# Hybrid decoder step with product-key experts, one core: h copied into PSUM in 36 of 64 expert steps, and projection heads, query norms, diagonals and late attention moved

## The reference, cut to what matters

```
q   = h @ w_pq, split in 8 heads x 2 halves x 128; each half normalised
s   = q . sub_keys                      (128 keys per half)
16 best of each half -> 16 x 16 sums -> 16 best: expert e = i1 * 128 + i2
gate = softmax(16 best sums)
act  = gelu(h . expert_u[e])            (16 experts per head and token)
out += gate * act * expert_v[e]         -> second layer norm -> y
```

## Time and profile before

| what | value |
|---|---|
| median of 3 runs | 4193.62 us |
| span of the profiled execution | 4435.8 us |
| POOL busy | 2465.2 us (56%) |
| DVE busy | 2799.8 us (63%) |
| PE busy | 2995.1 us (68%) |
| gathers of expert rows | 2 x 1024, and 16 for the sample |

### The profile page before, as it was taken

One profiled execution on the slowest core, in us unless ns is written; L12 is line 12 of the kernel. 1 busy time (PEld: TensorE's weight loads), 2 busy tenths in 40 slices (PEclk: granted clock), 3 DMA queues, 4 the chain that ended last, 5 costly groups with the idle time before them and its releaser, 6 DMA issues.

```text
span 4435.8 us, 41900 instructions
## 1 busy us (share of the span) xinstructions
PE 2995.1 (68%) x12168; PEld 1491.0 (34%) x12168; DVE 2799.8 (63%) x6694; ACT 917.6 (21%) x2005; POOL 2465.2 (56%) x2288
## 2 busy tenths in 40 slices
PE   5968877976866777866677778885666654444435
PEld 3546545645414433422223334441222221010001
DVE  6576851324665466668766766666776668657662
ACT  1423110233411244421111134331111110000000
POOL 1010110102576565676777777667777767777775
PEclk8988988966687877877888888767878877777777
DMA  6575983336699888899999999889999999999998
GB/s 234 182 310 218 386 328 104 106 126 215 230 360 348 313 312 285 306 345 359 370 378 386 362 358 354 326 309 332 380 376 375 382 357 338 354 362 360 348 342 310
DMA packets 422338, 1388.96 MB, mean 313 GB/s; under 512 B 46374, under 2 KB 124454, under 8 KB 409822
## 3 DMA queue, kind: packets, MB, share of 16 engines
q0 software_dynamic: 306432, 1216.48, 73.2%
q1 hardware_dynamic: 89390, 140.65, 9.4%
q10 hardware_dynamic: 26288, 29.15, 1.9%
HBM read 1333.57 MB, written 56.86 MB: 313 GB/s over the span
## 4 chain that ended last, share of the span: by engine, by line
POOL 35%; PE 15%; issue 15%; DMA 5%; DVE 4%; another core or an unknown queue 4%; DVEq 1%; ACT 0%; ACTq 0%; SPq 0%; PEldq 0%; POOLq 0%; PEld 0%
POOL st_rows L1525 35%; DMA st_rows<-in_peer_v,st_expert_v 4%; PE st_ps_q L1794 3%; PE st_ps_m L1804 3%; PE st_ps_q L1833 2%; PE st_ps_y L1878 2%; PE st_ps_t L1777 2%; DVE st_rows L2113 1%; PE st_ps_m L1810 1%; DMA st_rows<-in_peer_u,st_expert 1%; PE st_ps_m L1746 1%; PE st_ps_q L1797 1%; PE st_ps_s L1862 1%; DMA st_h<-scr_h 0%
## 5 line engine op out<-in xcount | busy, mean ns | idle before, releaser
L1878 PE MATMUL st_ps_y<-st_rows,st_diag 128*32 128x512 f32 x4096 | 1095.6, 658 | 730.7 <-DMA st_rows<-in_peer_v,st_expert_v 633.1
L1525 POOL DMA_INDIRECT st_rows<-in_peer_u,st_expert x1024 | 1191.3, 1163 | 645.4 <-issue 292.3
L2113 DVE CUSTOM_DVE_ANT_0 st_rows<-st_rows,st_h 128x1024 f32<-128x1024 f32 x1024 | 1218.1, 1223 | 394.4 <-DMA st_rows<-in_peer_u,st_expert 318.5
L1525 POOL DMA_INDIRECT st_rows<-in_peer_v,st_expert_v x1024 | 1137.5, 1111 | 509.6 <-issue 287.9
L1878 PEld LDWEIGHTS st_ps_y<-st_rows,st_diag 128*32 128x32 f32 x4096 | 199.9, 115 | 1585.9 <-issue 957.0
L602 PE MATMUL pd_ps<-pd_w,pd_xnT 128*128 128x256 f32 x1152 | 275.0, 399 | 24.8 <-ACT pd_stage L511 13.7
L1833 PE MATMUL st_ps_q<-st_shared 128*128 128x128 f32 (+3 forms) x1024 | 255.3, 412 | 8.4 <-issue 7.7
L424 POOL DMA_INDIRECT pd_kv<-in_cache_v,pd_rows x32 | 34.4, 1074 | 393.6 <-DVE pd_z L863 378.7
L602 PEld LDWEIGHTS pd_ps<-pd_w,pd_xnT 128*128 128x128 f32 x1152 | 227.8, 201 | 69.8 <-issue 37.3
L1862 PE MATMUL st_ps_s<-st_both,st_pick_tokens 128*128 128x32 f32 (+1 forms) x520 | 88.8, 322 | 213.6 <-issue 194.9
L2153 DVE TENSOR_TENSOR st_shared<-st_shared,st_ps_m 128x256 f32<-128x256 f32 (+5 forms) x176 | 73.2, 416 | 245.4 <-PE st_ps_m L1804 211.2
(11 more groups left out here) (326 smaller groups left out, 3878.4 us busy)
## 6 DMA issues: line engine op xcount, KB each, us to landing
st_shared<-in_w_pq_heads SPq DMA_DIRECT2D x32, 1024.0 KB
st_rows<-in_peer_u,st_expert POOLq DMA_INDIRECT x1024
st_rows<-in_peer_v,st_expert_v POOLq DMA_INDIRECT x1024
pd_w<-in_w_in SPq DMA_DIRECT2D x14, 1024.0 KB
scr_proj<-pd_stage ACTq DMA_DIRECT2D x8, 1152.0 KB
hs_step<-scr_factors SPq DMA_DIRECT2D x20, 416.0 KB
scr_score<-st_sc_out ACTq DMA_DIRECT2D x64, 130.0 KB
st_sc<-scr_score SPq DMA_DIRECT2D x64, 130.0 KB
```

Source lines behind the costliest of these rows:

```text
L1525: pool.indirect_dma_start(rows[n % R][:, :], None, src, bass.IndirectOffsetOnAxis(ap=idx, axis=0)).then_inc(row_loaded[n % R], 16)
L1878: ins = nc.tensor.matmul(ps_y[j * QUAD:(j + 1) * QUAD, c * 512:(c + 1) * 512], diag[k % 2][:, QS * j + q, :], rows[n % R][:, c * 512:(c + ...
L2113: nc.vector.tensor_tensor_reduce(out=rows[n % R][:, :], in0=rows[n % R][:, :], in1=hb, scale=1.0, scalar=0.0, op0=ALU.mult, op1=ALU.add, a ...
```

## The change

Four things.

1. h in PSUM. A step is free when neither attention nor mix uses ps_m in it. In free steps DVE's dots read h from ps_m in place of the SBUF copy. ACT copies h there (`copy_h`, two copies of 128x512) at the first free step and at each change of block: 10 times in all. PE's mix and attend wait for the last free step's dots before they write ps_m. Of the 64 steps 36 are free: 3, 6 to 9, 17, 21 to 29, 40, 41 and 45 to 63.
2. The table. Group 1: its 8 heads were scored four per step in steps 6 and 7, and are now scored two per step in 6 to 9. Group 2: all moved two steps on (attention 10 to 16, heads one per step 22 to 29). Group 3: attention in 10 steps of 8 slots (30 to 39) where it had 9 steps of 9 (28 to 36); heads two per step in 46 to 49 where they were one per step in 42 to 49. Where a step scores two heads, PE does the first ahead of values(k-1) and the second behind it.
3. query_norms is done for one head just ahead of its routing, and no longer for all the heads of the step that scores them.
4. value_inputs stands behind the tenth dot, and no longer behind the fourth.

```
-    plan = {1: (0, 3, 3, 6, 4), 2: (8, 7, 15, 20, 1), 3: (28, 9, 37, 42, 1)}
+    plan = {1: (0, 3, 3, 6, 2), 2: (10, 7, 17, 22, 1), 3: (30, 11, 41, 46, 2)}
...
+    FREE = [k not in ATTEND and k not in MIX for k in range(STEPS)]
+    H_COPY = [k for k in range(STEPS) if FREE[k] and (k % H == 0 or not FREE[k - 1])]
...
+            def copy_h(k):
+
+                b = k // H
+                act.wait_ge(h_loaded[b % 2], 16 * (b // 2 + 1))
+                act.wait_ge(dots_ready, k)
+                act.wait_ge(mix_read, mixes_before(k))
+                act.wait_ge(x_ready, tiles_before(k))
+                for n in range(2):
+                    nc.scalar.copy(ps_m[:, n * 512:(n + 1) * 512], h[b % 2][:, n * 512:(n + 1) * 512])
+                act.drain().then_inc(h_copied, 1)
...
-                for g, hd in SCORE.get(k, ()):
+                for g, hd in SCORE.get(k, ())[:1]:
                     copy_scores(g, hd)
                 weights(k)
+                if k + 1 in H_COPY and k not in MIX:
+                    copy_h(k + 1)
                 if k + 2 < STEPS:
                     exps(k + 2)
+                if k + 1 in H_COPY and k in MIX:
+                    copy_h(k + 1)
+                for g, hd in SCORE.get(k, ())[1:]:
+                    copy_scores(g, hd)
...
+                heads = SCORE.get(k, ())
+                for g, hd in heads[:1]:
                     score_head(g, hd)
                 if k > 0:
                     values(k - 1)
+                for g, hd in heads[1:]:
+                    score_head(g, hd)
                 spread_both(k)
...
+                if FREE[k]:
+                    dve.wait_ge(h_copied, copies_upto(k))
                 slots = ATTEND.get(k, ())
                 for s in range(K):
-                    dot(row_u(k, s), h[b % 2][:, :], act_in[k % 2][:, s:s + 1])
-                    if s == 3:
+                    dot(row_u(k, s), ps_m[:, :] if FREE[k] else h[b % 2][:, :], act_in[k % 2][:, s:s + 1])
+                    if s == 9:
...
-                if k in SCORE:
-                    query_norms(SCORE[k][0][0], tuple(hd for g, hd in SCORE[k]))
+                b, hd = divmod(k + 2, H)
+                if k + 2 < STEPS and GROUP_OF[b][0] > 0 and GROUP_OF[b][1] == 0:
+                    query_norms(GROUP_OF[b][0], (hd,))
                 if k + 2 < STEPS:
                     route(k + 2)
```

More of the change, by code:

```diff
@@ L1228, in stream @@
     read_at[SAMPLE_AFTER + 1] = SAMPLE_BLOCK
+    FREE = [k not in ATTEND and k not in MIX for k in range(STEPS)]
+    H_COPY = [k for k in range(STEPS) if FREE[k] and (k % H == 0 or not FREE[k - 1])]
+    copies_upto = lambda k: sum(c <= k for c in H_COPY)
+    mixes_before = lambda k: 1 + sum(x < k for x in MIX)
+    tiles_before = lambda k: TILE0[1] + sum(0 <= t < len(TILES[g]) for x in ATTEND if x < k for g, t in ATTEND[x])
+    last_free = lambda k: max((x for x in range(k) if FREE[x]), default=-1)
     with ExitStack() as ctx:
@@ L1316, in stream @@
         score_stored = [sem(f"score_stored{hd}") for hd in range(H)]
+        h_copied = sem("h_copied")
         h_stored, h_loaded, h_used = sem("h_stored"), [sem(f"h_loaded{j}") for j in range(2)], sem("h_used")
@@ L1743, in mix @@
                     pe.wait_ge(mix_read, b)
+                    free = last_free(next(x for x in MIX if MIX[x] == b))
+                    if free >= 0:
+                        pe.wait_ge(dots_ready, free + 1)
                 for n in range(2):
@@ L1764, in attend @@
                         pe.wait_ge(mix_read, mixed["n"])
+                    free = last_free(min((x for x in ATTEND if ATTEND[x][0] == (g, t)), default=0))
+                    if free >= 0:
+                        pe.wait_ge(dots_ready, free + 1)
                 def place(n):
```

## The result

The changed kernel takes 4148.03 us (median of 4 runs, 4141.25 to 4154.59), the kernel before 4194.13 us beside it (4 runs, 4182.05 to 4204.58): ratio 0.9896, 95% interval 0.9874 to 0.9919. So it is 46 us faster, in the range, but 72 us above my 4076; it went the way forecast, by 40% of the amount.

The account below looks back on a forecast made before the run. It took POOL as the bound, full with 32 gathers a step held by DVE's dots. Terms summed to -133 us, cut to -115 by a fifth off A, C and D: 4193.6 - 115 = 4079, stated as 4076; range 4005 to 4160.

Parts of the forecast that it names:

- A: Free steps without heads, 50 to 63: h in PSUM ends the hold on gathers, 48.3 to 43.5 us a step; -70 us.
- C: Other free steps (17, 21, 40, 41, 45): four of them gain 4.5 us each; -18 us.
- D: Steps 22 to 29, one head each: late scores take back most of the PSUM gain, 48.0 against 48.4 us; -3 us.
- B: Heads of group 1, two a step in 6 to 9: 214 us against 255 for the same work; -41 us.
- early attention of group 2: Attention moved to steps 10 to 16: still 9 slots a step, so no change; 0 us.
- E: Heads of group 3, two a step in 46 to 49: 212 us against 196; +16 us.
- F: Late attention, now ten steps with 8 slots instead of nine with 9; -12 us.
- G: Diagonals: value_inputs six dots later, so DVE no longer waits for PE's spread; -5 us.
- transfers bind anyway: Rival: the DMA can't keep 400 GB/s over whole steps, so A, C and D vanish; 4151 us, chance 0.14.
- lost lead: Steps 6, 22 to 29 and 46: a head's score is now used in the step that makes it, no longer ahead.
- the late h: Next block's h load stands behind a w_pq load waiting for PE's second head: steps 7 and 47 at 58 us.
- The slower rival: Scores 12 us later than assumed in each of ten steps make the change slower; 4229 us at 15; chance 0.07.

Follow-up runs that it names:

- e1: The kernel before, unchanged, profiled again on the slower kind of chip: 4481.34 us, where its median was 4467.27 us.
- e8: The kernel before, unchanged, profiled again on the faster kind of chip: 4178.03 us, where its median was 4195.75 us.
- e7: h in PSUM as changed, but table, heads, norms and diagonals as in the kernel before; faster kind of chip: ratio 0.9854 to the kernel before, 4128.20 us.
- e2: The same kernel as e7, on the slower kind of chip: ratio 1.0208 to the kernel before.
- e16: e2 with h kept in SBUF in steps that score a head; slower kind of chip: ratio 0.9869 to the kernel before.
- e18: The kernel of e16 again, slower kind of chip: ratio 0.9879 to the kernel before, 4425.53 us.
- e3: The changed kernel without h in PSUM (FREE False in every step), slower kind of chip: ratio 0.9989 to the kernel before.
- e6: The changed kernel with h kept in SBUF in steps that score a head; faster kind of chip: ratio 0.9880 to the kernel before.
- e5: The changed kernel, unchanged, timed again on the faster kind of chip: ratio 0.9911 to the kernel before, 4153.59 us.
- e12: The changed kernel with the diagonals behind the fourth dot again, slower kind of chip: ratio 1.0149 to the kernel before.
- e11: The kernel of e4 again, slower kind of chip: ratio 1.0155 to the kernel before.
- e4: The changed kernel with the next block's h loaded ahead of the next step's query weights; slower kind of chip: ratio 1.0171 to the kernel before.
- e14: The kernel of e4 again, on another chip of the slower kind: ratio 1.0167 to the kernel before.
- e17: e6 with h loaded ahead of the next step's query weights; slower kind of chip: ratio 0.9957 to the kernel before.

## Why the forecast was wrong

**Two steps failed.** One is the base of the sum: "The median is 242 us below that span, so without the profiler steps are shorter and nearer to the DMA's 42.1; I take a fifth off A, C and D". The profiler costs nothing that shows (e1, e8); the rows were like those of the other kind of chip. A fifth off three terms was a guess that came to 18 us, and B, from the same rows, got nothing off. The other is a term that was put at nothing: "The early attention of group 2 keeps 9 slots a step: 0". It cost 36 us, the largest miss of any term. The table has e8 as base. Steps are summed from one gelu to the next and rounded; "on A" is the changed kernel's profile minus e8, "PSUM alone" is e7 minus e8, so what the first has and the second lacks comes from the rest of the change. Stretches go by step number; e8's and e7's own heads and late attention lie in part in other ones.

| term, steps | forecast | on A | PSUM alone |
|---|---|---|---|
| A, 50 to 63 | -70 | -46 | -43 |
| B, 6 to 9 | -41 | -23 | -1 |
| "early attention of group 2: 0", 10 to 16 | 0 | +36 | -2 |
| C, 17 to 21 and 40 to 45 | -18 | -2 | -1 |
| D, 22 to 29 | -3 | +1 | -12 |
| E, 46 to 49 | +16 | +24 | 0 |
| F, 30 to 39 | -12 | -20 | -10 |
| G and all else in 1 to 5 | -5 | -4 | 0 |
| sum | -133 | -33 | -69 |

Outside the steps the changed kernel's profile is 3 us longer, which makes the -30.5 between the spans 4176.3 and 4145.8; the medians differ by 46. The -133 came down to -115 by the fifth, and to my 4076, 3 us below what the sum gives, for no reason that I gave. The measured 4148 lies 3 us from the 4151 of the rival "transfers bind anyway"; that is chance, since that price has A at nothing.

**A: mechanism right, base wrong.** The new steps were forecast at 43.5 us and take 42.7 (554 / 13). But the old ones took 45.6 on A, (315.5 + 277.5) / 13, and 48.3 in the earlier trace rows. POOL is held there too (u gathers in e8's steps 50 to 56: 1156 ns); its step was 3 us above what the transfers now allow, not 6. PSUM alone, e7 against e8, gives 43 us in steps 50 to 63.

**C and D: the transfers were the bound already.** In e8 steps 42 to 45 run at 409 GB/s, and steps 20 to 27, which have a head each, at 397 (steps 20 to 27 of e8, then of e7):

```profile
2046.00:2412.00 366.00, 277.88 (x1024) 113.34 (x1022) 265.52 (x722) 49.57 (x120) 289.15 (x253) 0.86 1.02 397
```

```profile
2045.00:2407.00 362.00, 277.68 (x1024) 113.32 (x1023) 264.10 (x723) 50.93 (x123) 241.73 (x256) 0.87 1.02 407
```

POOL is busy 47 us less in e7, and the stretch is 4 us shorter; in steps 42 to 45 nothing changes. There a free POOL is worth next to nothing. This is my rival "transfers bind anyway", true for the steps with a head on A, false for the pure ones. On B it is true in part: e2, e16 and e18 carry no hold in steps 50 to 63, e2 and e16 at 358 to 372 GB/s, and they gain 43, 17 and 29 us there against e1.

D's own new steps were right, 382 us for 22 to 29 against 384. But e8's eight steps with a head take 366, not the 387 of the earlier trace rows, so they are 16 us longer where I had a gain of 3. That the lost lead costs this fits its waits for scores, which the forecast put at 3 to 8 us and which average 11 (waits in 2147 to 2530); no run put the lead back alone:

```profile
DVE st_top L2027 <- DMA st_sc<-scr_score: 76.4, 7, 14.8
```

**B: right in its own steps, blind next to them.** Steps 6 to 9 were forecast at 214 us and take 201; the old ones take 225 in e8, not 255. But I gave the attention behind them nothing, and it takes 374.5 us in steps 10 to 16, where the kernel before needs 338.5 for its seven steps 8 to 14 (step 8: 44.2, its counterpart 10 now: 72.5). SP issues the first tile's loads 29 us into step 10 (start 1537). It has issued nothing since 1516.7: `load_pair` waits for `qT_used`, that is for PE to be done with the last head of group 1, since scores and attention share buffers. The change puts that head behind values(8), and PE ends it at 1565.6:

```profile
1516.34 0.38 SPq L1400 DMA_DIRECT2D st_sc<-scr_score  x1
1565.67 0.33 SPq L1379 DMA_DIRECT2D st_shared<-scr_kT  x1
```

```profile
1565.32 0.28 PE L1877 MATMUL st_ps_s<-st_one,st_shared 128*128 128x1 f32 x2
```

In e8 the last head ends at 1463.9, SP follows at 1464.0, and step 8 starts only at 1466. What comes behind the late loads (waits in 1537 to 1610):

```profile
POOL st_rows L1532 <- DVE st_act_in L2146: 29.4, 7, 17.3
DVE st_shared L2180 <- ACT st_shared L1651: 21.4, 1, 21.4
...
PE st_ps_q L1824 <- DMA st_shared<-scr_proj: 12.5, 1, 12.5
```

That the cost is not PSUM's is shown: e7 doesn't have it, and e3, without PSUM on B, does (SP's first load 32.5 us into step 10 and 1.4 us behind PE's last head; the step takes 69.8 us, step 8 of e1 51.3). That it is the place of the last head, and not the table otherwise, is read from the trace and the kernel; no run moved that head alone.

**E and the late h.** I gave 46 to 49 the times 54, 58, 50, 50; they take 41.8, 55.9, 62.7, 42.9: 203 us in all, where I had 212. E is 8 us too small because the old four take 179 us in e8, not 196. The first step, without lead, is not long, and steps 47 and 48 are. In e6, without the copy, step 48 takes 56.4 and 49 takes 51.3, together the same 107.6 (e5: 62.8 and 43.0, 105.8), and DVE waits 26.3 us for h directly: the load is late, not the copy. What loading h first is worth on A stays open, since no run there tried it.

**G.** e12 against e11 and the other versions on B differs by no more than their intervals: not resolved.

**The slower rival**, a lost lead of the scores, did not come: DVE's waits for st_sc in the changed kernel stay inside the 15 us that I had named:

```profile
DVE st_top L2027 <- DMA st_sc<-scr_score: 110.2, 12, 14.8
```

The versions nearest to the change (e4, e11, e12, e14) are slower on B all the same, by a mechanism that no rival had. The changed kernel itself was not run there, so my 0.07 for "slower" isn't tested by it.

## To carry to other kernels

Before sizing a change, set the profile's own time beside the timed median; if they differ by 6%, as here, the rows may be of another chip than the times, and every "it is full" must be checked again. Look for steps that already run at the highest rate of transfers seen anywhere: freeing the issuing engine gains only in the others. When work is moved to a later place on one engine, look for who waits for its end: here the loads of the next stage stood behind the last head by a shared buffer, and it cost 36 us that no term had.

## Not expected of the hardware

- Two chips differ by 6.5% for one program: 4196 against 4467 us, granted clock 0.811 (e8) and 0.780 (e1). Free steps with h in PSUM carry 396 and 409 GB/s on A (changed kernel), 358 to 372 on B (e2, e16). What makes the difference is open.
- On B, the end of a head is signalled up to 25 us after its last matmul starts while the gathers run unheld (transfers at 413 GB/s in the head shown), in 16 of 16 heads of e2 and none of e7. What in the chip stops PE stays open; its granted clock in that window is 0.65, over the span 0.759. With h in SBUF beside the heads most are on time (e16), though not all (e3, e17).
- Taking one input of the dot from PSUM frees POOL's gathers (0.94 us beside a dot in the rows above, 971 ns in the mean of steps 50 to 56) at 1218 ns a dot.
